# A two-block layer stack: where VectorE and ScalarE take the modulation rows of the first block

## The reference

```python
# first block: h + concat(attention, state space, linear recurrence) @ w_out
u = rms_norm(h, norm_g); proj = u @ w_in
q, k = rms_norm(q, q_g), rms_norm(k, k_g)          # 8 heads of 64
y_att = softmax(q k^T / 8 + decay, causal) v * silu(z_att)
y_ssd = rms_norm(ssd(silu(conv(xbc)), dt) * silu(z)) * g
# linear recurrence
a = exp(-8 r softplus(-lam)); mult = sqrt(-expm1(2 log a)); mult[0] = 1
h_t = a_t h_{t-1} + mult * (i * x_t);  y_lru = h * silu(z_lru)
h = h + concat(y_att, y_ssd, y_lru) @ w_out

# two decoder layers
mod = silu(c) @ w_ada + b_ada        # 1024 -> 6 * 1024, for each of the two layers
shift1, scale1, gate1, shift2, scale2, gate2 = split(mod, 6)
h = rms_norm(x) * (1 + scale1) + shift1
x = x + gate1 * (merged branches of (h @ w_in, h @ w_gate, w_branch) @ w_o)
h2 = rms_norm(x) * (1 + scale2) + shift2
x = x + gate2 * mixture_of_experts(h2)   # 32 experts, 2 for each token
```

## Time and profile before

| | us |
|---|---|
| median of three runs (2029.93 to 2034.96) | 2030.96 |
| the profiled execution | 2033.73 |
| its span | 2031.9 |

### The profile page before, as it was taken

One profiled execution on the slowest core, in us unless ns is written; L12 is line 12 of the kernel. 1 busy time (PEld: TensorE's weight loads), 2 busy tenths in 40 slices (PEclk: granted clock), 3 DMA queues, 4 the chain that ended last, 5 costly groups with the idle time before them and its releaser, 6 DMA issues.

```text
span 2031.9 us, 26836 instructions
## 1 busy us (share of the span) xinstructions
PE 1692.8 (83%) x12123; PEld 1156.8 (57%) x12123; DVE 528.4 (26%) x975; ACT 320.4 (16%) x637; POOL 41.4 (2%) x79
## 2 busy tenths in 40 slices
PE   8999999999999986665666699999999766665666
PEld 6886877887888842222222188878888322221223
DVE  5786872533111230000000045231022100000001
ACT  2332313312201020000000042212111100000001
POOL 0010100100000000000000001000000000000000
PEclk9999999999999997878888899999999887787888
DMA  7798845203446679999999932134484999999995
GB/s 260 251 371 332 314 163 187 94 3 125 138 151 258 239 315 430 431 433 431 431 431 431 415 131 84 44 125 150 141 337 159 402 433 429 431 431 431 431 429 243
DMA packets 88582, 582.38 MB, mean 287 GB/s; under 512 B 12024, under 2 KB 14864, under 8 KB 69392
## 3 DMA queue, kind: packets, MB, share of 16 engines
q1 hardware_dynamic: 79312, 530.16, 64.1%
q0 software_dynamic: 6912, 50.33, 6.4%
q10 hardware_dynamic: 2240, 0.11, 0.1%
HBM read 579.54 MB, written 1.05 MB: 286 GB/s over the span
## 4 chain that ended last, share of the span: by engine, by line
PE 47%; DMA 36%; DVE 1%; ACT 1%; issue 0%
PE ps L1305 13%; DMA expert_slots<-in_w_exp_down 13%; DMA expert_slots<-in_w_exp_gate 13%; DMA expert_slots<-in_w_exp_up 10%; PE ps L2101 8%; PE ps L2463 7%; PE ps L2114 4%; PE ps L2139 3%; PE ps L1308 1%; PE ps L1769 1%; PE ps L1781 1%; PE ps L1787 1%; PE ps L1739 1%; PE ps L1531 1%; PE ps L1262 0%; PE ps L2447 0%
## 5 line engine op out<-in xcount | busy, mean ns | idle before, releaser
L2463 PE MATMUL ps<-expert_slots,gathered 128*32 128x512 f32 x2048 | 313.3, 770 | 206.6 <-DMA expert_slots<-in_w_exp_up 119.8
L2463 PEld LDWEIGHTS ps<-expert_slots,gathered 128*32 128x32 f32 x2048 | 75.7, 136 | 434.7 <-issue 202.5
L1305 PE MATMUL ps<-h,ring 128*128 128x256 f32 x1216 | 275.5, 382 | 0.0
L1305 PEld LDWEIGHTS ps<-h,ring 128*128 128x128 f32 x1216 | 227.5, 190 | 37.0 <-issue 4.5
L2463 PE MATMUL ps<-expert_slots,gate_up_turned 128*32 128x512 f32 x1024 | 151.1, 744 | 95.6 <-DMA expert_slots<-in_w_exp_down 87.7
L2576 DVE TENSOR_TENSOR gate_up_rows<-silu_rows,ps 128x512 f32<-128x512 f32 x16 | 11.0, 688 | 763.7 <-issue 639.1
L2101 PE MATMUL ps<-h,ring 128*128 128x256 f32 x768 | 166.7, 379 | 0.0
L2101 PEld LDWEIGHTS ps<-h,ring 128*128 128x128 f32 x768 | 145.9, 190 | 19.8
L2463 PEld LDWEIGHTS ps<-expert_slots,gate_up_turned 128*32 128x32 f32 x1024 | 36.0, 133 | 199.3 <-DMA expert_slots<-in_w_exp_down 97.5
L262 PE MATMUL ps<-u,ring 128*128 128x256 f32 x640 | 145.2, 382 | 0.0
L262 PEld LDWEIGHTS ps<-u,ring 128*128 128x128 f32 x640 | 119.9, 190 | 20.4 <-issue 3.0
(11 more groups left out here) (466 smaller groups left out, 1607.7 us busy)
## 6 DMA issues: line engine op xcount, KB each, us to landing
expert_slots<-in_w_exp_up SPq DMA_DIRECT2D x32, 4096.0 KB, 33.5
expert_slots<-in_w_exp_down SPq DMA_DIRECT2D x32, 4096.0 KB, 33.9
expert_slots<-in_w_exp_gate SPq DMA_DIRECT2D x28, 4096.0 KB, 33.4
ring<-in_w_in SPq DMA_DIRECT2D x31, 2048.0 KB, 9.2
ada_ring<-in_w_ada POOLq DMA_DIRECT2D x48, 1024.0 KB, 7.7
ring<-in_w_gate SPq DMA_DIRECT2D x12, 2048.0 KB, 7.9
expert_slots<-in_w_exp_gate SPq DMA_DIRECT2D x8, 2048.0 KB, 7.6
ring<-in_w_branch SPq DMA_DIRECT2D x6, 2048.0 KB, 7.8
```

What stands on the lines that cost most here:

```text
L1305: ins = nc.tensor.matmul(k.ps[:, IN_BANK[t], 0:S], slab[:, j, c:c + w], k.h[:, j, :], start=j == 0, stop=j == ND - 1)
L2463: ins = nc.tensor.matmul(k.ps[r, bank, :], left[:, at + j, r], rows[:, i, j, :], start=at + j == 0, stop=last and j == 3)
```

## The change

Only places move; no instruction and no transfer is added or taken away. The sum of group 5 goes from behind tile 33 to behind tile 34. VectorE does fewer modulation rows ahead of the norms of k and q and at each place up to the linear recurrence; from row 91 on the places are the same. ScalarE takes the sum and the turn of group 10 before the square root and not behind it.

```diff
@@ -205,7 +205,7 @@
-ADA_AT = (19, 21, 23, 26, 30, 33, 36, 39, 41)
+ADA_AT = (19, 21, 23, 26, 30, 34, 36, 39, 41)
 ADA_STEPS = {t: [("sum", g)] for g, t in enumerate(ADA_AT)}
 ADA_STEPS |= {t + 1: [("turn", g)] for g, t in enumerate(ADA_AT)}
@@ -824,7 +824,7 @@
         ins.then_inc(sem.ssd_ready, 1)
-        f.scale(dve, 48)
+        f.scale(dve, 42)
@@ -940,7 +940,7 @@
             nc.vector.scalar_tensor_tensor(flat(t), flat(t), cols[gain], k.qk_square[:, n, :], ALU.mult, ALU.mult).then_inc(sem.qk_ready, 1)
-            f.scale(dve, 48 + 2 * (n + 1))
+            f.scale(dve, 42 + 4 * (n + 1))
@@ -965,7 +965,7 @@
                 lru_taps(k, f, dve, j)
-            f.scale(dve, 52 + (j + 1) * 5)
+            f.scale(dve, 50 + (j + 1) * 5)
@@ -1077,9 +1077,11 @@
         nc.scalar.activation(a[:, :, :], r[:, :, :], ACT.Exp, scale=-1.0).then_inc(sem.a_done, 1)
+        for step in LATE_STEPS[ND:2 * ND]:
+            f.take_sums(act, step)
         act.wait_ge(sem.square_done, 1)
         nc.scalar.activation(t[:, :, :], t[:, :, :], ACT.Sqrt).then_inc(sem.root_done, 1)
-        for step in LATE_STEPS[ND:]:
+        for step in LATE_STEPS[2 * ND:]:
             f.take_sums(act, step)
@@ -1093,7 +1095,7 @@
         step(nc.vector.tensor_scalar(rate, rate, 8.0, None, ALU.mult))
-        f.scale(dve, 86)
+        f.scale(dve, 85)
         dve.wait_ge(sem.z_att_silu, 1)
```

## The result

| | before | after |
|---|---|---|
| median, the runs of this comparison | 2032.38 us (7 runs, 2029.48 to 2035.68) | 2037.88 us (7 runs, 2036.92 to 2040.7) |
| the profiled execution, its span | 2033.73, 2031.9 us | 2036.92, 2035.1 us |
| TensorE, VectorE, ScalarE busy | 1692.8, 528.4, 320.4 us | 1703.3, 527.9, 320.5 us |

The ratio is 1.0031, 95% interval 1.0020 to 1.0043: slower by 4 to 9 us. Repeated later beside more runs of both it is 1.0018, interval 1.0009 to 1.0026 (12 runs against 29; medians 2038.18 and 2033.92). The change makes the kernel slower by 0.2 to 0.3%; the two intervals together leave 0.1 to 0.4%. TensorE's busy time grows by more than the launch does, since 6.6 us of its 10.5 fall between 760 and 1170 us, where the DMA engines are full (share 1.00) in both profiles.

A forecast was written before the change was run, and what follows sets the result against it. It took the chain of TensorE and DMA as the bound: 0.1 + 1.55 - 5.7 + 5.4 + 1.6 = +3.0 us, so 2036.7 profiled and, 2.8 lower, a median of 2034.0 us; range 2027 to 2038.

The forecast's parts named there:

- Norms, +0.1: k and q norms on VectorE: k starts earlier, but four rows between them end TensorE's wait for q +0.1 us later.
- Group 5's tile, 0: Group 5's sum one tile later, 33 to 34: ScalarE's copy is ready before its turn; 0, between -0.3 and +0.5 us.
- Group 8's sum, +1.55: TensorE behind tile 41: a late DMA piece now carries rows 70 and 71, which the sum needs; +1.55 us.
- Turn of group 10, -5.7: TensorE's wait for ScalarE's copy near 277 us and the half clock behind it go; -5.7 us, bounds -3.9 and -6.5.
- Row 90 and group 11's sum, +5.4 +1.6: VectorE waits about 4 us for row 90's piece, so TensorE waits at group 11's sum: +5.4 us, lower clock +1.6.
- The square root, 0: ScalarE's root behind group 10's copies: copies end about 277.9, its square only at 285.5, so the root loses nothing.
- Rival 1: Pieces land in 4.9 us and both new waits vanish, leaving -5.7 + 0.1: 2025.4 us; chance 0.24, a third of it whole.
- Rival 2: The wait at tile 41, group 8's sum, brings the lower clock too: +6.4 us, 2037.4; chance 0.12.
- rival 3: The q norm does come earlier, at 167.7, ending TensorE's wait and slow stretch, some -6.5 us: 2027.5; chance 0.02.

The follow-up runs named there:

- VectorE's part alone: The changed kernel with ScalarE's order of before (VectorE's batches and group 5's tile as changed); ratio 1.0040 to the kernel before, median 2041.89 us.
- with 86: The changed kernel with 86 rows, not 85, ahead of the attention's gate; ratio 0.9985 to the kernel before, median 2030.44 us.
- ScalarE's edit alone: The kernel before with only group 10 taken ahead of the square root on ScalarE; ratio 0.9976, median 2028.73 us.
- 85 alone: The kernel before with ScalarE's edit, and 85 rows, not 86, ahead of the attention's gate; ratio 0.9985, median 2030.71 us.
- the run without rows between the norms: The kernel before with ScalarE's edit, 42 rows ahead of the k norm, none between, ten behind the q norm; ratio 0.9959, median 2026.68 us.

## Why the prediction was wrong, point by point

I forecast +3.0 us and put 0.84 on less than 0.3%. The first comparison gave +6.3 us (0.31%), the second +3.7; 2037.88 is at the upper edge of my range. The direction was in the sum, but I called it no change, and one term was mis-sized. I also took 0.3% for what a measurement can tell; the interval of the first comparison is 0.12% to either side. That the end of the profiled pair shows +3.2 us is luck: only 1.0 of it is in the first block.

- **Norms, +0.1: right.** k at 165.46 (said 165.6), q at 171.89 (said 172.1 at most), TensorE's wait ends at 173.22 against 173.21.
- **Group 5's tile, 0: right.** No wait at either place.
- **Group 8's sum, +1.55: right place, too large.** 1.25 and 0.78 us in two profiles, 0.7 and 0.9 in the runs with VectorE's part alone and with 86, behind rows 70 and 71, whose piece took the 7.8 us of the earlier trace rows in the changed kernel and 7.3 in its repeat.
- **Turn of group 10, -5.7: the step that failed.** The wait did go, but its price was read from one execution. 3.86 us with half clock behind it is the high end of what this wait is; twice it was 2.0 to 2.2 with none. For the pair of profiles the measured terms close: 0.0 + 1.25 - 5.7 + 3.99 + 1.5 = +1.0, as 302.08 against 301.08. With -2.1 in place of -5.7 they give +4.6, between the 6.3 and 3.7 of the two comparisons; with -3.3, the mean of the three profiles, +3.4. ScalarE's edit alone measured about -5, so the mean over runs lies likely between the two sizes. That is as far as it is shown: the interval of that run, -3.1 to -6.9, holds -5.7 and not -2.1, and how often the half clock comes in the runs without a profile can't be seen.
- **Row 90 and group 11's sum, +5.4 +1.6: right place, the wait a quarter too large in two profiles.** VectorE waited 3.38 us ahead of row 90, not 4, since its piece was issued at 265.7, not 267.3, the pieces before it having let VectorE go on 1.5 to 2.2 us sooner than I took them; TensorE waited 3.99, and eight records took 1.5 us more at half clock (the earlier trace rows shows the like). In the run with VectorE's part alone the same program's rows ended at 292.0, where I had said 292.1, so this size too is one draw. Against the +3.0, the terms that I had too large here and at group 8 (by 1.8 us together) partly made up for the turn. From 286 on, the windows of TensorE in the changed kernel (start:end, length, busy, clock, DMA share, GB/s):

```profile
286.00:289.80 3.80, 0.00 (x0) 1.00 0.00 0
290.30:293.70 3.40, 3.40 (x13) 0.50 0.02 5
```

- **The square root, 0: right.** ScalarE's copies end at 277.4, the square at 283.2.
- **Rival 1 (pieces in time)** failed for this kernel, yet its condition came true in the run with 85 alone: 5.0 us for row 90's piece, issued ahead of the slab. **Rival 2** (half clock at group 8's sum) did not come; **rival 3** was excluded by the program's order, as the run without rows between the norms shows by doing what it only names; the block came 3.7 us earlier there, not 6.5.

More of the chance belonged above 0.3%, by my reckoning now about a third: a sum of +3, with the largest negative term from one execution and its lower bound (-3.9) already giving +4.8, leaves more than 0.12 above 6.1.

## What to carry to other kernels

When a wait is priced for removal, look for its size in more than one execution: of two engines that arrive nearly together the one profile shows one draw. Here the clock loss came whole behind a wait of 3.86 us (1.7 us lost) and not at all behind 2.16 and 1.99. When work is moved past a ring's boundary, count which instruction frees which slot and which sum needs the piece that lands in it; one row on the wrong side of such a boundary was worth 5 us and more in one setting and about 2, not clear of noise, in another, and the move of rows from ahead of the k norm did nothing for TensorE, since four rows then stood between the two norms.

## What the runs showed of the hardware that I had not expected

- With the same code ahead of it, the last block of the output product started at 296.96, 298.41 and 301.08 us in three executions, and the wait for the q norm behind rows that wait for DMA was between 4.4 and 6.3 us; with VectorE waiting only for ScalarE there it was 4.76 in each of five profiles.
- Half clock in the layers comes and goes between profiles of the same instructions there: at 402.9 and 1252.8 us in the changed kernel, where the profile before had none, near 1252 alone with 0.9 or 3.5 us of matmuls added, and for 3.4 us at 321 where the earlier trace rows had 6.8. Whether the shift of the first block sets it was not settled. TensorE by stretch in the changed kernel:

```profile
321.00:324.40 3.40, 3.40 (x10) 0.50 1.07 383
402.90:406.30 3.40, 3.40 (x47) 0.50 0.00 0
1252.80:1256.20 3.40, 3.40 (x36) 0.50 0.00 0
```

- Row 90's piece of 1 MB, issued 0.9 us ahead of the 2 MB slab, landed in 5.0 us; issued within 0.1 us of it, in 7.5 to 7.7; issued 0.2 us behind it (VectorE's part alone), in 9.3. Behind the slab another piece took 8.6 (267.1 and 266.4 us in the kernel with ScalarE's edit alone). An early issue is not enough by itself: in that kernel row 90's own piece, issued at 261.1 while the piece before it was under way until 264.7, took 7.8.
